# Memory values projected with the tokens stationary and the weights of all heads moving, in an encoder block on one core

## What is computed

```python
def memory_attention(q, memn, w_kv):
    kv = (memn @ w_kv).reshape(b, memn.shape[1], 2, M_HEADS, M_HEAD_DIM)
    mk, mv = kv[:, :, 0], kv[:, :, 1]
    logits = jnp.einsum('bshd,bmhd->bhsm', q, mk).astype(jnp.float32) * (d ** -0.5)
    p = jax.nn.softmax(logits, axis=-1)
    out = jnp.einsum('bhsm,bmhd->bshd', p.astype(mv.dtype), mv)
```

## Time and profile before

| | us |
|---|---|
| median of 3 runs | 717.54 |
| lowest, highest | 717.44, 718.22 |
| the profiled execution | 717.69 |
| its span in the trace | 715.9 |
| TensorE busy | 706.1 |
| VectorE busy | 426.2 |
| ScalarE busy | 311.7 |
| GpSimd busy | 231.6 |

### The profile page before, as it was taken

One profiled execution on the slowest core, in us unless ns is written; L12 is line 12 of the kernel. 1 busy time (PEld: TensorE's weight loads), 2 busy tenths in 40 slices (PEclk: granted clock), 3 DMA queues, 4 the chain that ended last, 5 costly groups with the idle time before them and its releaser, 6 DMA issues.

```text
span 715.9 us, 11698 instructions
## 1 busy us (share of the span) xinstructions
PE 706.1 (99%) x3885; PEld 589.5 (82%) x3885; DVE 426.2 (60%) x930; ACT 311.7 (44%) x721; POOL 231.6 (32%) x204
## 2 busy tenths in 40 slices
PE   8999999999999999999999999999999999999996
PEld 8988888888888888888888888888888887888885
DVE  6785256776754677775467777636676786322231
ACT  6752444445533445464334636434454554112210
POOL 5723132143433214343231434232234542222200
PEclk9999999999999999999999999999999999999999
DMA  9921211020052101105211110521130275514211
GB/s 298 299 60 31 58 39 51 1 59 2 1 153 53 36 23 31 28 0 147 59 29 30 29 29 0 147 60 30 30 122 2 63 238 181 155 59 125 81 53 42
DMA packets 79144, 52.53 MB, mean 73 GB/s; under 512 B 36080, under 2 KB 71936, under 8 KB 79104
## 3 DMA queue, kind: packets, MB, share of 16 engines
q1 hardware_dynamic: 79104, 52.06, 25.4%
HBM read 43.14 MB, written 8.91 MB: 73 GB/s over the span
## 4 chain that ended last, share of the span: by engine, by line
PE 94%; DVE 4%; ACT 1%; issue 1%; DVEq 0%; POOL 0%; ACTq 0%; POOLq 0%
PE acc L1462 18%; PE acc L1464 18%; PE acc L1463 17%; PE score L1462 4%; PE score L1463 3%; PE score L1464 3%; PE score L1656 3%; PE trans L1463 3%; PE trans L1464 3%; PE trans L1462 3%; PE score L1658 3%; PE trans L1677 2%; PE score L1734 2%; PE mixo L1462 2%; PE mixo L1463 2%; PE mixo L1464 2%
## 5 line engine op out<-in xcount | busy, mean ns | idle before, releaser
L1462 PE MATMUL acc<-x_hi,w_hi 128*128 128x512 f32 x544 | 217.5, 400 | 0.0
L1464 PE MATMUL acc<-x_hi,w_lo 128*128 128x512 f32 x544 | 213.8, 393 | 0.0
L1463 PE MATMUL acc<-x_lo,w_hi 128*128 128x512 f32 x544 | 212.5, 391 | 0.0
L905 POOL TENSOR_TENSOR w_lo<-w_raw,w_hi 128x512 fp32r<-128x512 f32 x66 | 85.7, 1319 | 173.3 <-ACT w_hi L592 154.6
L1464 PEld LDWEIGHTS acc<-x_hi,w_lo 128*128 128x128 f32 x544 | 102.1, 188 | 23.2
L1462 PEld LDWEIGHTS acc<-x_hi,w_hi 128*128 128x128 f32 x544 | 102.2, 188 | 20.1 <-issue 1.8
L1463 PEld LDWEIGHTS acc<-x_lo,w_hi 128*128 128x128 f32 x544 | 102.3, 188 | 19.1
L761 ACT ACTIVATE logits<-logits,stats_b 128x256 f32<-128x256 f32 (+3 forms) x64 | 52.6, 824 | 46.6 <-DVE stats_b L1267 46.6
L1259 DVE CUSTOM_DVE_ANT_0 logits<-score,b_bias 128x512 f32<-128x512 f32 (+1 forms) x96 | 53.5, 598 | 22.3 <-PE score L1658 18.6
L770 ACT ACTIVATE p_hi<-trans 128x512 fp32r<-128x512 f32 x56 | 32.6, 596 | 63.4 <-PE trans L1677 39.4
L1286 DVE TENSOR_TENSOR p_lo<-trans,p_hi 128x512 fp32r<-128x512 f32 x56 | 38.0, 689 | 29.4 <-ACT p_hi L770 29.0
(11 more groups left out here) (248 smaller groups left out, 1369.1 us busy)
## 6 DMA issues: line engine op xcount, KB each, us to landing
w_raw<-in_w_in SPq DMA_DIRECT2D x68, 256.0 KB, 3.4
mixed<-gates SPq DMA_DIRECT2D x9, 512.0 KB, 4.2
mix_raw<-mixed SPq DMA_DIRECT2D x8, 576.0 KB, 5.6
wo_raw<-in_w_out SPq DMA_DIRECT2D x8, 512.0 KB, 6.7
x_res<-in_x SPq DMA_DIRECT2D x8, 512.0 KB, 3.3
out_y<-y_row SPq DMA_DIRECT2D x16, 256.0 KB, 2.0
logits<-in_x SPq DMA_DIRECT2D x4, 512.0 KB, 8.1
wo_raw<-in_w_out SPq DMA_DIRECT2D x6, 256.0 KB, 5.7
```

The lines of the kernel that those rows point to most:

```text
L905: last = pool.tensor_tensor(w_lo[:, slot, cols], w_raw[:, slot, cols], w_hi[:, slot, cols].bitcast(F32), ALU.subtract)
L1462: pe.matmul(out, a_hi, b_hi, start=start, stop=False, skip_group_check=True)
L1463: pe.matmul(out, a_hi, b_lo, start=False, stop=False, skip_group_check=True)
L1464: return pe.matmul(out, a_lo, b_hi, start=False, stop=stop, skip_group_check=True)
```

## The change

The four key tiles come first (tiles 0 to 3) and keep their form, one bank each. The values are then four tiles of another kind (mem_value_tile, 4 to 7): a tile is two of the eight contraction steps, and all 512 value columns of w_kv. The memory's tokens are stationary (two blocks r of 128), the weights move, 512 columns at a time. All four tiles add into two banks, pre_acc[2 + r], so that a tile has 4 x 3 = 12 matmuls of 512 columns, and only the last one finishes both banks. The result has the tokens on the partitions; the transposes and the copies into mv_raw are gone. VectorE takes the two banks out in four instructions (mem_values), each with the tokens' factor as a scalar per partition, between normalise(2) and normalise(3). In before it took tiles 4 to 7 out one by one between the steps on x. The banks of the last transposes (those of a_v) move from numbers 22 to 25 to 20 to 23, and with them from score 1, score 2, trans 0, trans 1 to trans 0, trans 1, score 1, score 2. The loads of tiles 4 to 7 keep their size and places in the queue; they read rows of 512 columns.

```diff
--- before.py
+++ after.py
@@ -51,7 +51,7 @@
 MEM_TILES = 8
 PRE_RAW = 4
 PRE_ACC = 12
-PRE_T = 26
+PRE_T = 24
 
 
 BETWEEN = {
@@ -450,11 +450,14 @@
 
             def load_mem_tile(n):
 
-                col = (n // 2) * P + (n % 2) * 4 * P
                 full = raw_full[n] if n < 2 else mem_w_full[n - 2]
                 for c in range(2):
                     ks = slice(c * KT // 2, (c + 1) * KT // 2)
-                    sp.dma_start(raw_w[n][:, ks, :], w_mem_v[:, ks, bass.ds(col, P)]).then_inc(full, 16)
+                    if n < HEADS:
+                        src = w_mem_v[:, ks, bass.ds(n * P, P)]
+                    else:
+                        src = w_mem_v[:, 2 * (n - HEADS) + c, HEADS * P:2 * HEADS * P].rearrange("p (q n) -> p q n", n=P)
+                    sp.dma_start(raw_w[n][:, ks, :], src).then_inc(full, 16)
 
             def load_row(t):
                 sp.dma_start(x_raw[t], x_rows[:, t, :]).then_inc(rows_full[t], 16)
@@ -713,7 +716,7 @@
 
             def head(h, order):
                 def start():
-                    act.wait_ge(t_free, 22)
+                    act.wait_ge(acc_free, 8)
                     act.wait_ge(s_full, h * NS)
                     act.wait_ge(pt_done, h * NMIX)
                     act.activation(mk_hi[:, :], mk_raw[:, bass.ds(h, 1), :].rearrange("p a n -> p (a n)"), ACT.Copy)\
@@ -1100,8 +1103,17 @@
             def mem_tile(n):
 
                 dve.wait_ge(acc_full, n + 1)
-                out = mk_raw[:, n // 2, :] if n % 2 == 0 else mv_t[:, (n // 2) * MEM:(n // 2 + 1) * MEM]
-                dve.tensor_tensor(out, pre_acc[n % 4][:, 0:MEM], mem_rstd, ALU.mult).then_inc(acc_free, 1)
+                dve.tensor_tensor(mk_raw[:, n, :], pre_acc[n][:, 0:MEM], mem_rstd, ALU.mult).then_inc(acc_free, 1)
+
+            def mem_values():
+
+                dve.wait_ge(acc_full, MEM_TILES)
+                for r in range(2):
+                    for half in range(2):
+                        dve.tensor_scalar(mv_raw[:, 2 * half:2 * half + 2, r, :],
+                                          pre_acc[2 + r][:, half * MEM:(half + 1) * MEM]
+                                          .rearrange("p (h n) -> p h n", h=2), row_stats[:, r, 6:7], None, ALU.mult)\
+                           .then_inc(acc_free, 1)
 
             def shared_half(n, s):
 
@@ -1124,20 +1136,15 @@
                 mem_tile(n)
             normalise(0)
             mem_tile(3)
-            mem_tile(4)
             for b in range(2):
                 x_bank_lo(0, b)
             normalise(1)
-            mem_tile(5)
             for b in range(2, 4):
                 x_bank_lo(0, b)
-            mem_tile(6)
-            for b in range(2):
-                x_bank_lo(1, b)
-            mem_tile(7)
-            for b in range(2, 4):
+            for b in range(4):
                 x_bank_lo(1, b)
             normalise(2)
+            mem_values()
             normalise(3)
             shared_half(0, 0)
             for b in range(4):
@@ -1154,10 +1161,6 @@
             for i in range(2):
                 table(dve.tensor_copy(sinks.rearrange("p (t g i) -> p t g i", t=4, g=2)[:, :, :, i],
                                       sink_in.rearrange("p (g t) -> p t g", g=2)))
-            for v in range(2):
-                dve.wait_ge(t_full, 21 + v)
-                dve.tensor_copy(mv_raw[:, 2 * v:2 * v + 2, :, :].rearrange("p h a n -> p (h a n)"), pre_t[20 + v])\
-                   .then_inc(t_free, 1)
             dve.wait_ge(lam_exp, 1)
             table(dve.tensor_tensor(neg_lam, lam_exps[:, 1:2], lam_exps[:, 0:1], ALU.subtract))
             table(dve.tensor_scalar(neg_lam, neg_lam, -LAM_INIT, None, ALU.add))
@@ -1171,8 +1174,8 @@
             for v in range(4):
                 if v in (0, 2):
                     shared_half(v // 2, 1)
-                dve.wait_ge(t_full, 23 + v)
-                dve.tensor_copy(a_v[:, 4 * v:4 * v + 4, :].rearrange("p c n -> p (c n)"), pre_t[22 + v])\
+                dve.wait_ge(t_full, 21 + v)
+                dve.tensor_copy(a_v[:, 4 * v:4 * v + 4, :].rearrange("p c n -> p (c n)"), pre_t[20 + v])\
                    .then_inc(t_free, 1)
 
             def wo_lo_part(j):
@@ -1480,7 +1483,7 @@
                     pe.wait_ge(mem_rstd_made, 1)
                 pe.wait_ge(t_free, n - 1 if n < 14 else n - 3)
                 if n in (14, 15):
-                    pe.wait_ge(acc_free, n - 7)
+                    pe.wait_ge(acc_free, 2 * n - 22)
                 for j in range(2):
                     k = 2 * b + j
                     for par in range(2):
@@ -1503,8 +1506,6 @@
 
             def mem_tile(n):
 
-                if n >= 4:
-                    pe.wait_ge(acc_free, n - 3)
                 for k in range(KT):
                     if k == 0:
                         pe.wait_ge(*((w_lo_half, n) if n else (w_lo_first, 1)))
@@ -1513,8 +1514,27 @@
                     if n == 0 and k % 2 == 0:
                         pe.wait_ge(t_free, k // 2 + 1)
                     w = slice(k * P, (k + 1) * P)
-                    last = product(pre_acc[n % 4][:, 0:MEM], w_hi[:, n % 2, w], w_lo[:, n % 2, w], mem_hi[:, k, :],
+                    last = product(pre_acc[n][:, 0:MEM], w_hi[:, n % 2, w], w_lo[:, n % 2, w], mem_hi[:, k, :],
                                    mem_lo[:, k, :], k == 0, k == KT - 1)
+                last.then_inc(acc_full, 1)
+
+            def mem_value_tile(n):
+
+                kr = [(k, r) for k in range(2) for r in range(2)]
+                if n == HEADS:
+                    kr = [(k, r) for r in range(2) for k in range(2)]
+                for at_kr, (k, r) in enumerate(kr):
+                    if at_kr == 0:
+                        pe.wait_ge(w_lo_half, n)
+                    if (k, r) == (1, 0):
+                        pe.wait_ge(w_lo_done, n + 1)
+                    if n == HEADS and k == 0:
+                        pe.wait_ge(acc_free, 3 + r)
+                    w = slice(k * HALF, (k + 1) * HALF)
+                    rows = slice(r * P, (r + 1) * P)
+                    kt = 2 * (n - HEADS) + k
+                    last = product(pre_acc[2 + r], mem_hi[:, kt, rows], mem_lo[:, kt, rows], w_hi[:, n % 2, w],
+                                   w_lo[:, n % 2, w], kt == 0, kt == KT - 1)
                 last.then_inc(acc_full, 1)
 
             pe.wait_ge(const_made, 2)
@@ -1535,7 +1555,10 @@
             last.then_inc(gain_spread_made, 1)
             keep_busy_wide(BUSY[2])
             for n in range(MEM_TILES):
-                mem_tile(n)
+                if n < HEADS:
+                    mem_tile(n)
+                else:
+                    mem_value_tile(n)
                 if n == 1:
                     pe.wait_ge(mem_spread_made, 1)
                     for par in range(2):
@@ -1561,7 +1584,7 @@
                     if s == 0 and k == KT // 2:
                         pe.wait_ge(w_lo_done, n + 1)
                     if k == 0:
-                        pe.wait_ge(acc_free, n - 3 if s == 0 else n + 1)
+                        pe.wait_ge(acc_free, n - 7 if s == 0 else n + 1)
                     if n == 8 and k % 2 == 0:
                         pe.wait_ge(t_free, 4 + 4 * (2 * s + 1) + k // 2 + 1)
                     cols = slice(s * HALF, (s + 1) * HALF)
@@ -1573,10 +1596,10 @@
 
             def spread_shared(v):
 
-                pe.wait_ge(t_free, 19 + v)
+                pe.wait_ge(t_free, 17 + v)
                 for b in range(4):
                     c = 4 * v + b
-                    last = pe.transpose(pre_t[22 + v][:, b * P:(b + 1) * P], av_t[:, c * CHUNK:c * CHUNK + P],
+                    last = pe.transpose(pre_t[20 + v][:, b * P:(b + 1) * P], av_t[:, c * CHUNK:c * CHUNK + P],
                                         ident[:, :])
                 last.then_inc(t_full, 1)
 
@@ -1594,12 +1617,6 @@
             for b in range(2, 4):
                 spread_rows(3, b)
             shared_half(8, 1, first)
-            for v in range(2):
-                pe.wait_ge(t_free, 17 + v)
-                for b in range(4):
-                    last = pe.transpose(pre_t[20 + v][:, b * P:(b + 1) * P],
-                                        mv_t[:, (4 * v + b) * P:(4 * v + b + 1) * P], ident[:, :])
-                last.then_inc(t_full, 1)
             shared_half(8, 1, rest)
             pe.wait_ge(const_made, 6)
             for v in range(2):
```

## The result

| | before | after |
|---|---|---|
| median, us | 717.52 (12 runs, 716.93 to 718.31) | 719.58 (12 runs, 718.77 to 720.5) |
| the profiled execution's span, us | 715.9 | 717.3 |
| weight tile 4 (the first value tile after) begins, us of the trace | 22.34 | 22.08 |
| last transposes ahead of the heads begin, us of the trace | 66.14 | 67.57 |
| from the one to the other, us | 43.80 | 45.49 |

The changed kernel takes 1.0025 times as long, 95% interval 1.0016 to 1.0034, which is 1.15 to 2.44 us. The forecast was 719.0 us with a range of 717.8 to 719.9, and "slower by over 0.2%" at 0.49: the median lies 0.6 us above the forecast, inside the range. The ratio itself is above 0.2%, but its interval begins at 0.16%, so "over 0.2%" is likely and not certain.

A forecast was written before the change was run, and what follows sets the result against it. The prediction took TensorE's stream and its stops, with VectorE close beside it in the opening, as the bound. Delays of 2.25 us less 0.87 saved gave +1.4 on 717.69 (719.1) or the median (718.9): 719.0 us, range 717.8 to 719.9.

The forecast's parts named there:

- What bounds the kernel: Whole kernel: TensorE's stream of products and its few stops set the time; in the opening VectorE runs close beside it.
- The products: TensorE, value tiles: 48 products of 512 columns replace 96 of 256, saving 0.3 us, 0.07 to 0.08 us per tile.
- The eight transposes: TensorE, before the heads: removing the values' transposes and the break they make takes 0.87 us off the path.
- The stop at the second bank: First value tile: TensorE stands until VectorE takes key tile 3 out of bank 3, at 24.98 us; +1.29 us.
- The wait for the low half of the weights: First value tile: GpSimd's low half comes 0.1 to 0.2 us late, lost inside the longer wait for the bank.
- Up to the third pair: VectorE's x_lo and normalise up to the third pair of rows: delay shrinks as tile 5's take-out goes; +0.87 us.
- The take-outs: VectorE between normalise(2) and normalise(3): four added instructions at 0.35 us each, +1.4 us, bounds 1.36 to 1.58.
- The sum: At the start of the heads: 2.25 us of delay less 0.87 for the transposes, +1.4 us, coming through whole.
- Waits absent: Opening, rival: the added waits don't come and TensorE's own work sets the time; 716.5 us, chance 0.10 with half absent.
- Weights late: Value tiles' loads, rival: weights arrive late and ScalarE waits for them; 720.5 us, chance 0.04.
- The clock: TensorE behind the two 1.2 us stops, rival: clock falls to 1.2 GHz for some 3 us; 722 us, chance 0.04.

## Why the prediction was right, and where its sizes were off

**What bounds the kernel.** Right. TensorE's stream and its waits for VectorE made the whole difference; the pace of the heads is 0.229 us as before, the granted clock 1.00, and no DMA is late.

**The products.** Mis-sized. Predicted was a saving of 0.3 us. 48 x 0.234 = 11.23 us against 96 x 0.118 = 11.31 leave 0.08. The price was borrowed from the shared tile, where x moves and the weights are stationary; in the value tiles it is the other way round. A nearer row stood in the trace of before, in the output projection, where w_hi and w_lo serve in some of the products; the names are what is written, what moves, what is stationary:

```profile
610.03 0.39 PE L1463 MATMUL trans<-wo,mix_hi 128*128 128x512 f32 x1
...
611.16 0.39 PE L1462 MATMUL score<-w_hi,mix_hi 128*128 128x512 f32 x1
...
611.86 0.39 PE L1462 MATMUL score<-wo,mix_hi 128*128 128x512 f32 x1
```

The three with w_hi and w_lo moving are (611.86 - 611.16) / 3 = 0.233 us apart, the five before them, with the weights in wo moving, (611.16 - 610.03) / 5 = 0.226. So whether weights or rows of x move isn't by itself what sets the pace. The estimate from the Trainium skill (TensorE: Matmul & The Clock Gate, section "Back-to-back issue gap"), 0.12 us, came nearer, though 0.234 us is above its 518 cycles, which it gives for a matmul by itself. The error hardly touched the sum, because only the 0.08 us of one value tile were in it.

**The eight transposes.** Right: 0.87 us predicted, 0.87 us measured by putting eight back.

**The stop at the second bank.** Predicted 1.29 us, measured 1.38, and 1.20 come back with other banks, where 0.19 us of another wait appears. The bank was free at 24.32 + 0.42 = 24.74, which is 2.66 us into the tile (2.64 predicted). The restart took 0.05 us instead of 0.1, and the six products behind it 1.50 instead of 1.38: 4.21 in place of 4.12. The wait for the low half of the weights, called 0.1 to 0.2 us and hidden, shows as 0.36 us instead of 0.23 from the row at 22.55 to that at 22.91, and is hidden in the longer stop. It costs 0.19 us once that stop is gone.

**Up to the third pair.** Predicted +0.87 us, measured +1.02. 0.09 of the difference is carried over from the stop, 0.06 is the value tile that was 0.02 us shorter and not 0.08.

**The take-outs.** Predicted 1.4 us with bounds of 1.36 and 1.58; measured (46.47 - 44.90) = 1.57, 0.39 each, and 0.39 more for each one that was added. The choice of the cheaper neighbour failed: the dearer row, the form with a scalar per partition, was the right one. (The mean of 0.48 us used with it isn't in that row; the trace's list of groups has it, 476 ns.) The rule of the Trainium skill (VectorE: DVE Perf Modes, section "The TRN2 errata") gave 1.57 us, and this case agrees with it.

**The sum.** +1.69 us instead of +1.4 (unrounded 1.38): 0.15 from the third pair and 0.17 from the take-outs, which is the term that was sized too small. The last transposes come 2.44 us later, the second bank costs 0.13 more (0.92 us from 52.41 to 53.33 against 0.79 in the earlier trace rows), and 0.87 comes off. The medians are 2.06 us apart, of which 0.37 isn't in the opening; the interval of 1.15 to 2.44 us covers 1.69, so nothing more is claimed. The spans differ by 1.4 us because the trace of after began its tile 4 0.26 us sooner, and that agreement with the forecast is chance.

**The rivals.** Waits absent: not in this kernel, but 717.05 us when they are taken away, with a gain of 1.05 us of opening where 1.17 had been priced. The 0.3 us of products in that price were not on the path, and the 0.34 us of tile 5's take-out, which were, had been left out. Weights late: not seen. The clock: not in this kernel, seen behind stops of 2.03 and 2.81 us at a price of 1.4 to 1.6 us, about half of the 3 us that the prediction gave it.

## What to carry to other kernels

When work moves to another engine's side of a loop, price the take-out at the place where it lands. The same four instructions cost 1.57 us where VectorE had no gap and 0.5 us in a gap of which they could use 1.07 us; as two on ScalarE, which stood idle, they cost next to nothing. A result that fills two banks at once asks for banks whose last readers are long done: look at what stands in front of the take-out in its engine's queue, not at the number of banks. And take the price of a new instruction from a row with the same form and the same buffers in the same roles, wherever in the trace it stands, even if a cheaper row of the same size is nearer.

## What the runs showed of the hardware

- The place of buffers changes the pace of products. Three weight buffers moved by 32 bytes took the heads' products from 0.229 to 0.2333 us, in the stretch that was read, and the kernel from 719.6 to 724.9 us (724.2 us when moved the other way), two and a half times the loss of the change itself. The place isn't all: with the buffers unmoved a shared tile ran at 0.2335 us in one version and at 0.2295 in before.
- Products of 512 columns with w_hi or w_lo moving were 0.233 to 0.234 us apart, whatever the place of these buffers, and products with wo moving 0.226 in the stretch of before shown above; the mechanism is open.
- A stop of TensorE of 2.03 us was followed by the 1.2 GHz level, at a cost of some 1.6 us; one of 1.25 us at the same place of the program was not.
